# Input projection of a two-block transformer kernel: four panels multiplied by the unnormalised input

## The chip, the cores and the metric

The kernel is one program on one core of a Trainium2 chip. A core has a matrix engine (TensorE, PE in the profile), a vector engine (VectorE, DVE), a scalar engine (ScalarE, ACT), a general engine (GpSimd, POOL) and a sequencer that issues most transfers (SyncE, SP). They run side by side and wait for each other through semaphores. The metric is the device time of one execution in microseconds (us), the median of several.

## The reference, cut to what matters

The kernel computes two transformer blocks over 512 tokens of width 1024. Only the head of the first one matters here: the input is normalised, multiplied by one wide weight matrix, and the parts of the product go into two attentions.

```python
def rms_norm(x, g):
    xf = x.astype(jnp.float32)
    y = xf * lax.rsqrt(jnp.mean(xf * xf, axis=-1, keepdims=True) + EPS)
    return (y * g.astype(jnp.float32)).astype(x.dtype)
...
        h = rms_norm(x, g_mix_pre[l])
        proj = h @ w_in[l]
        q_f, k_f, v_f, f_logit, q_c, k_c, v_c = jnp.split(proj, splits, axis=-1)
        log_f = jax.nn.log_sigmoid((f_logit + b_fgate[l]).astype(jnp.float32))
        o_f = fox_attention(...)
        o_c = chunked_rel_attention(...)
        o_f = rms_norm(o_f.reshape(B, S, FOX_WIDTH), g_fox_out[l])
        o_c = rms_norm(o_c.reshape(B, S, CHUNK_WIDTH), g_chunk_out[l])
        mix = jnp.concatenate([o_f, o_c], axis=-1) @ w_out[l]
        x = x + rms_norm(mix, g_mix_post[l])
```

## The kernel before

The activations lie transposed: a chunk of x is 128 channels by 512 tokens, and there are 8 chunks. Every product is made of three fp32r matmuls (lines 1029 to 1031): each operand is split into a rounded high part and the low rest, and high times high, high times low and low times high are added up. The weights come as panels of 128x1024 (512 KB), one panel for one output chunk: SP loads a panel into one of two slots of `stage`, ACT rounds it into `WH` (line 1763), POOL subtracts to get `WL` (line 820) and counts it in `s_split`. The third and fourth panel of this projection go into a buffer of their own, `WX`. The load of panel p waits until panel p-2 is split.

At the start SP issues x in three parts (2, 2 and 4 chunks), the first constants, the vectors (gains, biases), panels 0 and 1, and, when all of x is there, the other constants (`con`), the condition and the gate weights. ACT squares the chunks of x (line 1791), DVE adds the squares (line 2485), PE sums them over the channels with a matrix of ones (lines 1157 and 1160), ACT takes the logarithm and the exponential (lines 1806 and 1809), which gives the reciprocal root. DVE scales a chunk (line 2515), ACT rounds it (line 1815), DVE makes its low part (line 2509): the pair is `H`. Meanwhile PE multiplies constants that nobody reads (`warm`, line 1136), 40 ahead of the sum and 14 behind it.

Then PE runs the input projection (`project`): output chunks 0 and 1 together, chunk of H by chunk of H, then chunks 2 to 15 one after the other, 24 matmuls each. Chunks 0 and 1 use the banks G[0] and G[1], 2 and 3 use ST and AD, all later ones G[0] and G[1] in turn. ACT copies a finished chunk rounded to `QKH` (line 1836), DVE makes `QKL` (line 2730) and so frees the bank. Beside the chunks each engine has other work, at fixed places between them: after chunk 0 ACT computes a SiLU of the condition between two loads of its function table (lines 2185 and 1800), after chunk 3 DVE subtracts over a bias table that SP loads when H is done (line 2943), and at every even chunk from 4 on DVE takes two pieces of another weight matrix (line 2574).

The values and gates follow, and then self attention, 64 steps over 16 heads. A step s is one head and one block of 128 queries; PE computes the scores of two heads together (lines 1344 to 1350, `score_pair`), DVE takes the maximum, ACT the exponential, PE transposes (line 1263, `turn`), ACT and DVE make the two parts of the transposed weights, and from step 8 on PE also multiplies them by the values (`weigh`). PE's order is written out in `attention`: pairs 0 and 2, then for each s `turn(s)`, `score_pair(s+4)` at even s, and what is to be weighed. The other attentions have `warm(O[1], 4)` ahead of each of the first four steps, self attention has none.

## Time and profile before

| | us |
|---|---|
| median of 3 runs | 2083.13 |
| lowest and highest run | 2078.95, 2084.5 |
| the profiled execution, its own time | 2083.59 |
| its span, first to last instruction | 2081.8 |
| mean granted TensorE clock | 0.994 |

The rows further down are of this one execution. A page begins with the busy time of each engine; then come a table of the span in 40 slices, groups of instructions, and, asked of the trace, the instructions of a stretch in order of time. "Granted clock" is the share of TensorE's full speed that the chip gave it: 1.00 is 2.4 GHz and 0.50 is 1.2 GHz.

### The profile page before, as it was taken

How to read it: one execution, taken by the hardware profiler on the slowest of the kernel's cores; microseconds unless marked ns; L12 is line 12 of the kernel's file. 1: busy time of each engine (PE TensorE's matmuls, PEld its weight loads, DVE VectorE, ACT ScalarE, POOL GpSimd, SP SyncE). 2: the span in 40 equal slices, each digit the busy share in tenths (PEclk: the TensorE clock that was granted, in tenths of full speed). 3: DMA queues.
4: the chain of work that ended last, by engine and by line, in shares of the span. 5: the costliest groups of instructions: out<-in, count | busy, mean ns of one | idle time of the engine just before them, and what ended most of it. 6: DMA issues, size and time to landing. Idle time of an engine off the chain costs nothing.

```text
span 2081.8 us, 27861 instructions
## 1 busy us (share of the span) xinstructions
PE 2048.6 (98%) x9868; PEld 1685.8 (81%) x9868; DVE 1115.9 (54%) x1704; ACT 864.7 (42%) x1413; POOL 938.0 (45%) x478
## 2 busy tenths in 40 slices
PE   9999999999999999999999999999999999999997
PEld 7877887888888888787778888888777888888887
DVE  4525735236777776763485533434576635334345
ACT  5326864354222222533386323223475653232333
POOL 3444585552545454434244344444445752444443
PEclk9998999999999999999999999999999999999999
DMA  6530152224566664264223233333222032333332
GB/s 208 192 110 21 42 182 82 80 61 142 172 219 235 226 228 140 91 241 153 76 61 97 61 96 96 100 92 101 81 91 72 1 102 61 91 101 93 99 97 85
DMA packets 70325, 238.40 MB, mean 115 GB/s; under 512 B 7776, under 2 KB 11232, under 8 KB 70112
## 3 DMA queue, kind: packets, MB, share of 16 engines
q1 hardware_dynamic: 70240, 237.26, 35.4%
q8 instruction: 54, 0.88, 0.2%
q14 instruction: 31, 0.25, 0.0%
HBM read 231.20 MB, written 2.10 MB: 112 GB/s over the span
## 4 chain that ended last, share of the span: by engine, by line
PE 52%; issue 18%; POOL 7%; DVE 5%; ACT 3%; DMA 1%; POOLq 0%; DVEq 0%; ACTq 0%; SPq 0%
PE bank L1029 16%; PE bank L1031 16%; PE bank L1030 16%; POOL WL L820 5%; PE bank L1178 1%; PE bank L1151 1%; DMA stage<-panels 1%; DVE bank L2599 1%; PE bank L1263 1%; DVE acc L2485 1%; PE bank L1136 1%; POOL CW L967 0%; DVE x L2603 0%; DVE CPT L3060 0%; ACT CPT L2301 0%
## 5 line engine op out<-in xcount | busy, mean ns | idle before, releaser
L820 POOL TENSOR_TENSOR WL<-stage,WH 128x1024 fp32r<-128x1024 f32 x256 | 634.0, 2477 | 891.6 <-ACT WH L1763 886.4
L1763 ACT ACTIVATE WH<-stage 128x1024 fp32r<-128x1024 f32 x256 | 271.5, 1061 | 810.1 <-PE bank L1031 795.4
L1029 PE MATMUL bank<-H,WH 128*128 128x512 f32 (+1 forms) x1132 | 438.0, 387 | 3.2 <-DVE H L2509 2.2
L1031 PE MATMUL bank<-H,WL 128*128 128x512 f32 (+1 forms) x1132 | 437.0, 386 | 0.0
L1030 PE MATMUL bank<-H,WH 128*128 128x512 f32 (+1 forms) x1132 | 437.0, 386 | 0.0
L2839 DVE TENSOR_TENSOR Y<-bank,Y 128x512 f32<-128x512 f32 x328 | 215.8, 684 | 94.6 <-PE bank L1031 93.9
L1029 PE MATMUL bank<-HID,WH 128*128 128x512 f32 (+1 forms) x688 | 264.3, 384 | 0.1
L1030 PE MATMUL bank<-HID,WH 128*128 128x512 f32 (+1 forms) x688 | 264.2, 384 | 0.0
L1031 PE MATMUL bank<-HID,WL 128*128 128x512 f32 (+1 forms) x688 | 264.2, 384 | 0.0
L1029 PEld LDWEIGHTS bank<-H,WH 128*128 128x128 f32 x1132 | 212.6, 188 | 48.1 <-issue 4.0
L1031 PEld LDWEIGHTS bank<-H,WL 128*128 128x128 f32 x1132 | 212.6, 188 | 43.2
L1030 PEld LDWEIGHTS bank<-H,WH 128*128 128x128 f32 x1132 | 212.6, 188 | 42.9 <-issue 0.2
L2825 DVE SCALAR_TENSOR_TENSOR t<-bank,t 128x512 f32<-128x512 f32 x64 | 44.3, 692 | 266.9 <-ACT t L2086 266.8
L2574 DVE SCALAR_TENSOR_TENSOR ahead<-ahead,cond 128x1024 f32<-128x1024 f32 x102 | 175.5, 1771 | 9.0 <-DMA ahead<-ada 9.0
L2829 DVE TENSOR_TENSOR HID<-t,HID 128x512 fp32r<-128x512 f32 x86 | 121.5, 1412 | 65.9 <-ACT HID L2091 65.9
L1029 PEld LDWEIGHTS bank<-HID,WH 128*128 128x128 f32 x688 | 129.3, 188 | 25.7 <-POOL WL L820 0.3
L1031 PEld LDWEIGHTS bank<-HID,WL 128*128 128x128 f32 x688 | 129.3, 188 | 25.7
L1030 PEld LDWEIGHTS bank<-HID,WH 128*128 128x128 f32 x688 | 129.3, 188 | 25.6
L2730 DVE SCALAR_TENSOR_TENSOR QKL<-bank,QKH 128x512 fp32r<-128x512 f32 x40 | 27.4, 690 | 94.6 <-ACT QKH L1836 90.9
L2091 ACT ACTIVATE HID<-t 128x512 fp32r<-128x512 f32 x86 | 54.2, 630 | 57.3 <-DVE t L2825 51.6
L2740 DVE TENSOR_REDUCE stat<-bank 128x1 f32<-128x128 f32 (+3 forms) x112 | 52.7, 474 | 29.6 <-PE bank L1350 25.6
L1136 PE MATMUL bank<-onesr,identr 128*128 128x512 f32 x238 | 64.3, 418 | 1.2 <-DVE onesr L2920 1.2
(489 smaller groups left out, 3576.0 us busy)
## 6 DMA issues: line engine op xcount, KB each, us to landing
stage<-panels SPq DMA_DIRECT2D x296, 512.0 KB, 3.6
ahead<-ada SPq DMA_DIRECT2D x102, 512.0 KB, 5.3
RAW<-panels SPq DMA_DIRECT2D x18, 512.0 KB, 4.1
apiece<-ada SPq DMA_DIRECT2D x10, 512.0 KB, 5.3
x<-xT SPq DMA_DIRECT2D x3, 1024.0 KB, 8.4
CS<-QKH SPq DMA_DIRECT2D x18, 128.0 KB, 2.3
outT<-x SPq DMA_DIRECT2D x16, 128.0 KB, 1.7
CS<-QKL SPq DMA_DIRECT2D x12, 128.0 KB, 2.4
```

The lines of the kernel that those rows point to most:

```text
L820: pool.tensor_tensor(low_of(p, slot), stage[:, slot, :], high_of(p, slot).bitcast(F32), ALU.subtract).then_inc(s_split, 1)
L1029: pe.matmul(out, wh, rh, start=start, stop=False)
L1030: pe.matmul(out, wh, rl, start=False, stop=False)
L1031: return pe.matmul(out, wl, rh, start=False, stop=stop)
L1136: pe.matmul(out[:, :], identr[:, :], onesr[:, :].rearrange("p (a b) -> p a b", a=1).to_broadcast([P, 4, P]), start=True, stop=True)
L1763: act.activation(high_of(p, slot), stage[:, slot, :], ACT.Copy).then_inc(s_hisplit, 1)
L2091: act.activation(HID[:, slot, j, 0, :], t[:, j, :], ACT.Copy).then_inc(sm["high"], 1)
L2574: dve.scalar_tensor_tensor(source, source, 1.0, cond[:], ALU.mult, ALU.mult, accum_out=adac[:, column])\
L2740: dve.tensor_reduce(stat[:, b:b + 1], score_bank(name, s)[:, 0:w], AX, ALU.max, negate=True)\
L2825: ins = dve.scalar_tensor_tensor(t[:, j, :], up_banks[j][:, :], 0.0, t[:, j, :], ALU.max, ALU.mult)
L2829: dve.tensor_tensor(HID[:, slot, j, 1, :], t[:, j, :], HID[:, slot, j, 0, :].bitcast(F32), ALU.subtract).then_inc(sm["split"], 1)
L2839: dve.tensor_tensor(Y[:, m, :], (T + O)[m % 4][:, :], Y[:, m, :], ALU.add)\
```

## The change

The change has three parts.

**Input projection.** ACT and DVE first split x itself, times the gain, into H (`raw_high`, `raw_low`). PE multiplies panels 0 to 3 by this unnormalised H (`project_in`). The sum of squares goes between the products of panel 2. Chunks 0 to 3 are then multiplied by the reciprocal root per token in their banks (`scale_raw`, on DVE) before they are copied out. H is overwritten with the normalised x chunk by chunk as PE has used it, and output chunks 4 to 15 are computed from that. The warmers ahead are 26, and none stand behind the sum. Chunk 2 now lies in AD and chunk 3 in ST.

**Loads.** SP issues panel 0, the vectors, the first part of x, panel 1, the rest of x, the first constants. Panels 6 and 7 are loaded ahead of the bias table and not behind it and two pieces. The bias table waits for the normalised H.

**Self attention.** Six constant matmuls ahead of `turn(0)` and two ahead of `turn(2)`.

```diff
+SELF_CONSTANTS = (6, 0, 2, 0)
...
-            for at, part in enumerate(X_PARTS):
+            def load_x(at):
+
+                part = X_PARTS[at]
                 sp.dma_start(x[:, part.start:part.stop, :],
                              xT[part.start * P:part.stop * P, :].rearrange("(c p) t -> p c t", p=P))\
                     .then_inc(s_x[at], 16)
-                if at == 0:
-                    sp.dma_start(con[:, 0:CON["mask"]], cons[:, 0:CON["mask"]]).then_inc(s_ones, 16)
-            sp.dma_start(vec[:], vecs).then_inc(s_vec, 16)
-            for slot in range(2):
-                sp.dma_start(stage[:, slot, :], panels[slot]).then_inc(s_stage[slot], 16)
+
+            sp.dma_start(stage[:, 0, :], panels[0]).then_inc(s_stage[0], 16)
+            sp.dma_start(vec[:], vecs).then_inc(s_x[0], 16)
+            load_x(0)
+            sp.dma_start(stage[:, 1, :], panels[1]).then_inc(s_stage[1], 16)
+            load_x(1)
+            load_x(2)
+            sp.dma_start(con[:, 0:CON["mask"]], cons[:, 0:CON["mask"]]).then_inc(s_ones, 16)
             sp.wait_ge(s_x[2], 16)
...
-            plain(2, 6)
-            sp.wait_ge(s_h, row(MAKES, "x")[1])
+            plain(2, 8)
+            sp.wait_ge(s_h, before(MAKES, "x") + KC)
             sp.dma_start(Y[:, 0:4, :].rearrange("p a b -> p (a b)"), bias).then_inc(s_bias, 16)
             load_piece(0)
             load_piece(1)
-            plain(6, 8)
...
+            def project_in():
...
+                half = KC // 2
+                for p in range(2):
+                    pe.wait_ge(s_split, p + 1)
+                    for k in range(half):
+                        input_chunk("x_raw", k)
+                        product(p, G[p], k)
+                for k in range(half, KC):
+                    input_chunk("x_raw", k)
+                    for p in range(2):
+                        last = product(p, G[p], k)
+                        if k == KC - 1:
+                            last.then_inc(s_used, 1)
+                pe.wait_ge(s_split, 3)
+                for k in range(half):
+                    product(2, own_bank("w_in", 2), k)
+                    if k == 1:
+                        pe.wait_ge(s_ones, 16)
+                        mean_square("x")
+                pe.wait_ge(s_split, 4)
+                pe.wait_ge(s_log, first_of(LOG, "x") + 1)
+                for k in range(half):
+                    product(3, own_bank("w_in", 3), k).then_inc(s_raw, 1)
+                for k in range(half, KC):
+                    first, second = product(2, own_bank("w_in", 2), k), product(3, own_bank("w_in", 3), k)
...
+                for c in range(4, 6):
+                    chunk_of(c, "w_in", c, c % 2, H[:, :, 0, :], H[:, :, 1, :], S, "x" if c == 4 else None, evicted=c - 3)
+                with pe.Fori(3, 8) as i:
+                    for j in range(2):
+                        chunk_of(i * 2 + j, "w_in", i * 2 + j, j, H[:, :, 0, :], H[:, :, 1, :], S)
...
-                    if s < 4 and name != "self":
-                        warm(O[1], 4)
+                    if s < 4:
+                        warm(O[1], SELF_CONSTANTS[s] if name == "self" else 4)
...
-            warm(AD, 40)
-            pe.wait_ge(s_ones, 16)
-            mean_square("x")
-            warm(AD, 14)
-            project("w_in", 16, "x")
+            warm(AD, 26)
+            project_in()
...
+            used(PANEL0["w_in"], 0)
+            evacuate_scaled(0)
             for m in range(KC):
+                if m == 2:
+                    used(PANEL0["w_in"] + 1, 1)
+                if m < KC - 1:
+                    act.wait_ge(s_raw, m + 1)
+                else:
+                    act.wait_ge(s_used, 4)
                 high_chunk("x", m, scaled_in, hh, lambda m: col("zero"))
...
+            high_near(0)
+            for c in range(1, 4):
+                evacuate_scaled(c)
+                high_near(c)
...
+            def scale_raw(c):
+
+                dve.wait_ge(s_used, PANEL0["w_in"] + c + 1)
+                dve.tensor_tensor(own_bank("w_in", c)[:, :], own_bank("w_in", c)[:, :], rstd[:, :], ALU.mult)\
+                    .then_inc(s_qscaled, 1)
...
             await_rstd("x", added=True)
+            scale_raw(0)
+            evacuate_low("w_in", 0, QKH[:, 0, :], QKL[:, 0, :], 64 ** -0.5)
             make_scaled("x", xc, vcol("g_mix_pre"), hl, zero)
             dve.memset(RG[:].bitcast(F32), 0.0)
             dve.memset(RB[:].bitcast(F32), 0.0).then_inc(s_pad, 1)
             for c in range(16):
-                evacuate_low("w_in", c, QKH[:, c, :], QKL[:, c, :], 1.0 if c // 4 % 2 else 64 ** -0.5)
+                if 1 <= c < 4:
+                    scale_raw(c)
+                if c:
+                    evacuate_low("w_in", c, QKH[:, c, :], QKL[:, c, :], 1.0 if c // 4 % 2 else 64 ** -0.5)
```

What stands in a row on ACT before, from the reciprocal root to the copy of chunk 1 (line 1815 rounds H, 1763 a panel, 1836 copies an output chunk; the waits are semaphores):

```order
L1809 ACTIVATE bank<-logs 128x512 [waits mean_squares_log]
L1815 ACTIVATE H<-bank,vec 128x512 [waits scaled,vectors_loaded,ones_loaded]
L1815 ACTIVATE H<-bank,vec 128x512 [waits scaled] x4
L1763 ACTIVATE WX<-stage 128x1024 [waits panel0_loaded]
L1815 ACTIVATE H<-bank,vec 128x512 [waits scaled] x2
L1763 ACTIVATE WX<-stage 128x1024 [waits panel1_loaded]
L1815 ACTIVATE H<-bank,vec 128x512 [waits scaled]
L1763 ACTIVATE WH<-stage 128x1024 [waits panel0_loaded,panel_used]
L1836 ACTIVATE QKH<-bank 128x512
L2185 ACT_TABLE_LOAD
```

The same place on ACT now (1865 rounds the normalised H, 1811 a panel, 2247 copies a scaled output chunk):

```order
L1859 ACTIVATE bank<-logs 128x512
L1811 ACTIVATE WH<-stage 128x1024 [waits panel0_loaded,panel_used]
L2247 ACTIVATE QKH<-bank 128x512 [waits raw_product_scaled]
L1865 ACTIVATE H<-bank,vec 128x512 [waits scaled,raw_chunk_used] x2
L1811 ACTIVATE WH<-stage 128x1024 [waits panel1_loaded,panel_used]
L1865 ACTIVATE H<-bank,vec 128x512 [waits scaled,raw_chunk_used] x5
L1865 ACTIVATE H<-bank,vec 128x512 [waits scaled,panel_used]
L2264 ACT_TABLE_LOAD
L2264 ACTIVATE cond<-cond 128x1024 [waits condition_loaded]
L1848 ACT_TABLE_LOAD
L2247 ACTIVATE QKH<-bank 128x512 [waits raw_product_scaled]
```

The SiLU and its two table loads still stand ahead of the copy of chunk 1, and that copy now stands behind the whole of H.

What stands in a row on DVE now, from the end of H to the first pieces (2592 makes the last low parts of H, 3017 multiplies a chunk by the root, 2813 makes a low part and frees a bank, 3048 is the subtraction over the bias table, 2657 takes a piece):

```order
L2592 SCALAR_TENSOR_TENSOR H<-bank,vec,H 128x512 [waits input_high] x2
L3031 MEMSET RG 40x512 [waits input_split]
L3032 MEMSET RB 104x512
L3017 TENSOR_TENSOR bank<-bank,rstd 128x512 [waits panel_used,cond_ready]
L2813 SCALAR_TENSOR_TENSOR QKL<-bank,QKH 128x512 [waits chunk_high_evacuated]
L3017 TENSOR_TENSOR bank<-bank,rstd 128x512 [waits panel_used]
L3042 TENSOR_TENSOR wgateL<-wgate,wgateH 128x192 [waits gate_weights_high]
L3048 TENSOR_TENSOR Y<-Y 128x2048 [waits bias_loaded]
```

There the multiplication and the low part alternate for chunks 1, 2 and 3, and the subtraction over the bias table stands between the low parts of chunks 3 and 4.

What stands in a row on PE now at the start of self attention (1187 is a constant matmul, 1401 the last product of a score pair, 1395 the first of the next one):

```order
L1401 MATMUL bank<-maskr,identr 128x128 x2
L1187 MATMUL bank<-onesr,identr 128x512 [waits values_evacuated]
L1187 MATMUL bank<-onesr,identr 128x512 x5
L1395 MATMUL bank<-QKH 128x384 [waits self_exp]
```

Before, no constant stood there: the transposition followed the score pair at once.

## Rows read from the trace of the kernel before

**Rows 1.** The page: span, and busy us (share) xinstructions of two engines

```profile
span 2081.8 us, 27861 instructions
PE 2048.6 (98%) x9868; PEld 1685.8 (81%) x9868; DVE 1115.9 (54%) x1704; ACT 864.7 (42%) x1413; POOL 938.0 (45%) x478
```

**Rows 2.** Timeline of PE, start: start us, us, engine, line, op, out<-in, count [idle before]

```profile
1.25 12.19 PE L1136 MATMUL bank<-onesr,identr 128*128 128x512 f32 x40 [1.25 <-DVE onesr L2920]
13.71 1.10 PE L1157 MATMUL bank<-acc,con 128*128 128x512 f32 x2 [0.27 <-DVE acc L2485]
14.64 1.02 PE L1160 MATMUL bank<-sq,con 128*128 128x512 f32 x2
...
19.65 0.47 PE L1029 MATMUL bank<-H,WH 128*128 128x512 f32 x1 [0.79 <-DVE H L2509]
...
52.41 0.39 PE L1029 MATMUL bank<-H,WH 128*128 128x512 f32 x1
```

**Rows 3.** Timeline of ACT, start

```profile
15.70 0.69 ACT L1806 ACTIVATE logs<-bank,eps 128x512 f32<-128x512 f32 x1 [0.31 <-PE bank L1160]
16.42 0.60 ACT L1809 ACTIVATE bank<-logs 128x512 f32<-128x512 f32 x1
...
31.76 0.58 ACT L1836 ACTIVATE QKH<-bank 128x512 fp32r<-128x512 f32 x1
32.36 1.28 ACT L2185 ACT_TABLE_LOAD   x1
33.66 1.06 ACT L2185 ACTIVATE cond<-cond 128x1024 f32<-128x1024 f32 x1
```

**Rows 4.** Timeline of DVE, start

```profile
19.42 0.75 DVE L2515 SCALAR_TENSOR_TENSOR bank<-x,vec,bank 128x512 f32<-128x512 f32 x1
...
20.73 0.75 DVE L2515 SCALAR_TENSOR_TENSOR bank<-x,vec,bank 128x512 f32<-128x512 f32 x1
...
32.38 0.69 DVE L2730 SCALAR_TENSOR_TENSOR QKL<-bank,QKH 128x512 fp32r<-128x512 f32 x1 [2.72 <-ACT QKH L1836]
...
42.97 2.28 DVE L2943 TENSOR_TENSOR Y<-Y 128x2048 f32<-128x2048 f32 x1
```

**Rows 5.** Timeline of POOL, start

```profile
31.93 2.41 POOL L820 TENSOR_TENSOR WL<-stage,WH 128x1024 fp32r<-128x1024 f32 x1 [2.34 <-ACT WH L1763]
```

**Rows 6.** Transfers issued in the first 60 us: count, KB each, median us to landing

```profile
stage<-panels SPq DMA_DIRECT2D x10, 512.0 KB, 3.7
...
x<-xT SPq DMA_DIRECT2D x1, 1024.0 KB, 8.4
Y<-bias SPq DMA_DIRECT2D x1, 1024.0 KB, 5.6
```

**Rows 7.** Windows of 1 us: length, PE busy (x), granted clock, DMA share, GB/s

```profile
162.00:163.00 1.00, 0.00 (x0) 1.00 0.91 318
165.00:166.00 1.00, 1.00 (x5) 0.50 0.00 0
...
181.00:182.00 1.00, 1.00 (x6) 0.80 0.00 0
351.00:352.00 1.00, 0.00 (x0) 1.00 0.00 0
```

**Rows 8.** Timeline of PE, start of self attention

```profile
161.56 0.44 PE L1350 MATMUL bank<-maskr,identr 128*128 128x128 f32 x2
163.45 0.30 PE L1263 MATMUL bank<-con,t 128*128 128x128 f32 x1 [1.45 <-ACT t L1988]
...
165.24 0.43 PE L1263 MATMUL bank<-con,t 128*128 128x128 f32 x1
...
170.78 0.69 PE L1350 MATMUL bank<-maskr,identr 128*128 128x128 f32 x2
...
185.41 0.44 PE L1350 MATMUL bank<-maskr,identr 128*128 128x128 f32 x2
...
196.35 0.44 PE L1350 MATMUL bank<-maskr,identr 128*128 128x128 f32 x2
```

More of the change, by code:

```diff
@@ L513, in own_bank @@
         def own_bank(name, c):
-            return [ST, AD][c - 2] if name in JOINT and c in (2, 3) else G[c % 2]
+            if name in JOINT and c in (2, 3):
+                return ([AD, ST] if name == "w_in" else [ST, AD])[c - 2]
+            return G[c % 2]
         def q_panel(i):
@@ L1031, in three, with chunk_of @@
                 return pe.matmul(out, wl, rh, start=False, stop=stop)
-            def chunk_of(p, name, c, slot, high, low, width, fresh=None, part=range(KC)):
+            def chunk_of(p, name, c, slot, high, low, width, fresh=None, part=range(KC), evicted=None):
                 wh, wl = high_of(p, slot), low_of(p, slot)
@@ L1039, in chunk_of @@
                 else:
-                    if part[0] == 0:
+                    if evicted is not None:
+                        freed(pe, name, evicted)
+                    elif part[0] == 0:
                         bank_free(pe, name, c)
@@ L1830, in evacuate, with evacuate_high @@
                         act.activation(dest(i * 2 + j), G[j][:, :], func, scale=scale).then_inc(s_free, 1)
-            def evacuate_high(name, dest, scale, width=S, after=None):
-                for c in range(row(PROJ, name)[1]):
+            def evacuate_high(name, dest, scale, width=S, after=None, chunks=None):
+                for c in chunks or range(row(PROJ, name)[1]):
                     used(PANEL0[name] + c, c % 2)
```

65 lines of the change are left out of this document (49 added, 16 removed).

## The prediction, made before the changed kernel was run

> **What bounds the kernel now.** The page says it first: PE is busy for 98% of the span [rows 1], so only what shortens PE's own time, or closes one of its few gaps, moves the end. I read two stretches. The first is the start in the timeline of PE: constants and the sum of squares up to 18.9 us, the first useful product at 19.65, and from there a matmul each 0.227 us without a gap. 144 of them are six output chunks, and the seventh (chunk 6) begins at 52.41 [rows 2]: 32.76 us, or 5.46 per chunk. The second is the start of self attention, where the windows show the granted clock: PE does nothing from 162 to 163, and from before 165 until about 181.4 (a window at 0.80 is two fifths of slow time) the clock is 0.50, which is 1.2 GHz, though PE is busy all the time [rows 7]. PE waits there for ACT's first exponential until 163.45 [rows 8].
>
> **Part 1, the projection.** Chunk 6 is the first that the change leaves as it was: from it on each chunk costs PE the same 5.44 us with ACT and DVE idle in between, so the gain of this part is 52.41 less the time at which chunk 6 can begin now. The changed start, step by step:
>
> - Start. Panel 0 is now the first transfer: some 3.7 us [rows 6] after 0.74, then ACT 1.06 (any copy of 128x1024, as the SiLU's) and POOL 2.41 [rows 3, 5], so split near 8.0. The 26 constants last longer: 40 took 12.19 [rows 2], where the later ones run each 0.227, so 14 fewer end 3.2 earlier, near 10.1. The first product starts there, 9.5 us ahead of before. Panels 0 and 1 are 48 matmuls, 10.9 us, and end at 21.0. Raw H costs DVE 0.66 a chunk and keeps ahead of that.
> - Panel 2. SP waits for all of x. Its last part, 1 MB, took 8.4 us [rows 6]; issued near 3.3 behind somewhat more, it lands at 12. Then SP issues four transfers of 0.4 us each (constants, condition, gates, panel 2): panel 2 goes out at 13.4 with 1 MB ahead of it. Its landing takes between 3.7 (a panel alone) and 8.4; I take 5.0, nearer to the first and to the 5.6 that a whole MB takes [rows 6], so 18.4. ACT 1.06 and POOL 2.41 give 22.0. PE waits 1.0 us. **This is the softest term: every microsecond that the panel lands later or earlier moves all that follows, down to a gain of 1.0.**
> - The root. Two chunks of product are 1.4 us, the sum of squares is 1.95 (13.71 to 15.66) [rows 2], so it ends at 25.4. Logarithm 0.69, and now two exponentials of 0.60 where one stood [rows 3]: DVE has the root at 27.4, against 17.0 before.
> - Normalised H. DVE first multiplies chunk 0 by the root, ACT splits panel 4 and copies chunk 0, DVE makes the low part: 0.7 + 1.1 + 0.6, less overlap, ends at 29.6. Eight chunks of H then cost DVE 1.31 each (19.42 to 20.73) [rows 4]: 10.5 us, and with the last tail H is ready at 40.8. PE meanwhile does panels 2 and 3 until 34.9, and chunk 4, whose last product must wait for the last of H, until 41.6: 1.2 us of waits.
> - Chunk 5 writes over bank G[1], where chunk 1 still lies. Its copy stands on ACT behind the last of H (40.0) and behind the table load 1.28, the SiLU 1.06 and the second load 1.28 [rows 3]. ACT copies at 43.5 in 0.58, DVE's low part 0.69 [rows 4] frees the bank at 44.9. **PE waits 3.3 us.** This is the new wait of the change; the SiLU had stood under running products before.
> - Chunk 6 needs five freed banks. DVE, from 44.9: chunks 2 and 3 take 0.69 + 0.58 + 0.69 each with hand-overs, to 49.2; then the subtraction over the bias table, 2.28 [rows 4], to 51.4; then chunk 4's low part, to 52.1. The bias table is issued at 40.9 and lands 5.6 later [rows 6], at 46.5, in time; with two more pieces in flight it has 2.7 us to spare. Panel 6 is split only after ACT has copied chunk 3 (48.5): 49.5, and POOL 2.41 makes 52.0. Both say 52.2, while chunk 5 has ended at 50.4.
>
> So chunk 6 begins at 52.2 against 52.41: **0.2 us gained**. The 9.5 us of the early start go into waits of 1.0, 1.2, 3.3 and 1.8 and the 1.95 of the sum, which now lies between useful products. Loading panels 6 and 7 ahead counts nothing: they land long before ACT can round them, at 48.5. The pieces come later on DVE but are asked for at the same distance as before.
>
> The Trainium skill's page ScalarE: Activation LUTs says under "What ACT_TABLE_LOAD costs" that a switch is 1283 ns plus a drain of about 1380 ns. The trace agrees with the first number, not with the second: the SiLU starts 0.02 us after its load ends [rows 3]. By the page the chain through two loads would be 2.8 us longer, an estimate from its figure.
>
> **Part 2, the constants in self attention.** Six constants cost 6 x 0.227 = 1.36 us and stand in a gap: PE ends its second pair at 162.0 and the transposition starts at 163.45 [rows 8]. They first wait for ACT's copy of the values, which I put at 162.2 at the latest, so they end at about 163.55, 0.1 late. Two more, 0.45, stand where nothing waits: they cost their time. What they may return is the clock. If it stays at 1.00:
>
> - From 165.24 to 170.78 [rows 8] PE ran without a gap at 1.2 GHz: 5.5 us become 2.8. Less 0.45 and 0.1, this saves 2.2.
> - From the pair of step 8 to that of step 16, 14.63 us (170.78 to 185.41); the same distance one group later, at full clock and gapless, is 10.94 (185.41 to 196.35) [rows 8]. This saves 3.7. The early group has some 1.1 us fewer products by the values in it, and against them waits of about 1 us for DVE and ACT, which the slow clock had hidden; I take them as equal.
>
> Together **5.9 us**, all on PE's path, and what follows (memory, later layers) hangs on the same semaphores and moves with it.
>
> **The sum.** 2083.59 (the profiled execution, 0.46 above the median of the three runs) less 0.2 less 5.9 is 2077.5; against the median, 2077.0. That is 0.29%, right at the 0.3% (6.2 us) below which a measurement of this kernel can't tell it from no change.
>
> **The rivals.**
>
> - *The clock falls all the same.* For it: the six constants are followed by some 9 us in which PE runs only short transpositions and half-height score products, and at 1.2 GHz just such work, with PE busy, did not bring the clock back until products by the values had run. Against it: at 351 PE stood for over 1 us and the clock stayed [rows 7], and groups with the same mix hold it. If it falls two or three microseconds later, the gain is 0 to 3: 2080 to 2083.5.
> - The Trainium skill's page TensorE: Matmul & The Clock Gate says under "Part 4: PE-mode transpose" that a transposition does not count as PE-busy in the same way. By this rule the rival above holds, at its own time; the slow stretch agrees with it.
> - *The loads do better.* If panel 2 lands by 17.4, PE does not wait for it and everything up to chunk 6 is 1.0 earlier; with shorter hand-overs on ACT and DVE perhaps 2.3: 2074.7 to 2076.
> - *The new wait ahead of chunk 5 costs the clock.* PE stands for 3.3 us there; 1.45 us after light work were enough at 162. At the start of the program the slow phase cost 12.19 - 40 x 0.227 = 3.1 us [rows 2]. Chunk 5 has 1.8 us of slack before chunk 6, so 1.3 net: 2078.3.
> - *Slower.* The same mechanism at its worst: the clock falls in that wait and stays down as long as in self attention, some 17 us [rows 7], half of which is 8.5, less the slack 6.7; and the constants buy nothing. 2083.1 + 6.7 = 2089.8. It decides from the point where the slow phase outlasts chunk 5 by more than two chunks.
>
> **How the numbers follow.** Forecast 0.60 (2075.3 to 2079, panel 2 landing within 1.5 us of mine), clock falls all the same 0.15, loads do better 0.12, wait costs the clock but briefly 0.08, slower 0.05. Range: I leave out the slower case and the edges of its neighbours, 2074.5 to 2083.0. Faster by over 0.3% (below 2076.9): all of "better", half of the forecast, 0.42. Within 0.3%: the other half, the late fall and the brief one, 0.53. Slower by over 0.3%: 0.05.
>
> **What the profile after would show.** First product at 10.1. Waits of PE ahead of panel 2 (1.0, on POOL), at the end of chunk 4, ahead of chunk 5 (3.3, on DVE's low part of chunk 1) and ahead of chunk 6 (1.8), which starts at 52.2; DVE's subtraction over the bias table at 49.2. Self attention: granted clock 1.00 from 162 to 185, and the pair of step 16 some 6 us earlier. I am wrong if chunk 6 starts more than 2 us from 52.2, or if the clock shows 0.50 anywhere between 45 and 185.

## The result

| | before | changed |
|---|---|---|
| median of 20 runs each, us | 2080.09 | 2084.71 |
| lowest and highest run | 2077.21, 2084.5 | 2082.52, 2086.47 |
| profiled execution, its own time | 2083.59 | 2083.43 |
| its span | 2081.8 | 2081.5 |
| mean granted clock | 0.994 | 0.996 |

The ratio is 1.0019, 95% interval 1.0013 to 1.0025: slower by 0.19%, which is within the 0.3% of "no change", but 7.7 us above my 2077.0 and outside the range. The two profiled executions are alike to 0.2 us, the medians are not. The reason stands in the list of the 20 times: the runs of before lie in two groups, 12 of them from 2077.2 to 2080.5 and 8 from 2082.7 to 2084.5, and the execution whose trace I read was of the upper one. So were two of the three times that I had.

### The profile page after: what moved, and what is told of

It reads as the page before. It is cut to its first block, busy times and chain, and to the rows that moved or that the text cites. A ratio compares the mean times of both kernels' runs of the same rounds, so it can differ in the third digit from the quotient of the medians.

```text
span 2081.5 us, 27853 instructions
## 1 busy us (share of the span) xinstructions
PE 2042.0 (98%) x9848; PEld 1677.9 (81%) x9848; DVE 1126.8 (54%) x1716; ACT 871.4 (42%) x1422; POOL 939.8 (45%) x478
## 4 chain that ended last, share of the span: by engine, by line
PE 55%; issue 15%; POOL 6%; DVE 5%; ACT 4%; DMA 1%; POOLq 0%; DVEq 0%; SPq 0%; ACTq 0%
PE bank L1037 17%; PE bank L1038 17%; PE bank L1039 17%; POOL WL L828 4%; DMA stage<-panels 1%; PE bank L1202 1%; PE bank L1229 1%; PE bank L1314 1%; DVE acc L2568 1%; PE bank L1187 1%; DVE bank L2682 0%; POOL CW L975 0%; DVE CPT L3165 0%; ACT CPT L2384 0%; DVE Y L2922 0%
## 5 line engine op out<-in xcount | busy, mean ns | idle before, releaser
L1038 PEld LDWEIGHTS bank<-HID,WH 128*128 128x128 f32 x688 | 129.3, 188 | 25.4
L1187 PE MATMUL bank<-onesr,identr 128*128 128x512 f32 x218 | 58.4, 413 | 1.4 <-DVE onesr L3003 1.3
```

Source lines behind the costliest of these rows:

```text
L1038: pe.matmul(out, wh, rl, start=False, stop=False)
L1187: pe.matmul(out[:, :], identr[:, :], onesr[:, :].rearrange("p (a b) -> p a b", a=1).to_broadcast([P, 4, P]), start=True, stop=True)
```

## The profile of the changed kernel

In these lines a timeline row is: start us, us, engine, line, operation, out<-in, count [idle before <-what ended it]. The page is nearly that of before [rows 1]: PE is 6.6 us less busy by its records, DVE 10.9 and ACT 6.7 us more (H is now made twice, and four chunks are scaled in their banks).

```profile
span 2081.5 us, 27853 instructions
PE 2042.0 (98%) x9848; PEld 1677.9 (81%) x9848; DVE 1126.8 (54%) x1716; ACT 871.4 (42%) x1422; POOL 939.8 (45%) x478
```

**The start.** Timeline of PE, all rows with idle time up to chunk 6 and, at 26.16, the end of the sum of squares. They answer to [rows 2].

```profile
1.25 7.76 PE L1187 MATMUL bank<-onesr,identr 128*128 128x512 f32 x26 [1.25 <-DVE onesr L3003]
9.39 0.47 PE L1037 MATMUL bank<-H,WH 128*128 128x512 f32 x1 [0.39 <-DVE H L3011]
13.11 0.50 PE L1037 MATMUL bank<-H,WH 128*128 128x512 f32 x1 [2.10 <-DVE H L3011]
23.80 0.50 PE L1037 MATMUL bank<-H,WX 128*128 128x512 f32 x1 [0.69 <-POOL WX L828]
...
26.16 1.02 PE L1211 MATMUL bank<-sq,con 128*128 128x512 f32 x2
41.42 0.50 PE L1037 MATMUL bank<-H,WH 128*128 128x512 f32 x1 [0.35 <-DVE H L2592]
46.65 0.77 PE L1037 MATMUL bank<-H,WH 128*128 128x512 f32 x1 [3.34 <-DVE QKL L2813]
55.40 0.49 PE L1037 MATMUL bank<-H,WH 128*128 128x512 f32 x1 [0.34 <-POOL WL L828]
```

PE's wait of 2.10 at 13.11 is for the low part of the third chunk of raw H. ACT's high part of it came late, since ACT had waited until 7.56 for the first part of x, then rounded panel 1, and waited again until 10.38 for the second part. And the low part itself was slow: of the two instructions in the row of DVE that follows the first took 1.83 us instead of 0.75, beside POOL's split of panel 1 (timelines of DVE and of POOL; what that means comes further down).

```profile
11.23 2.49 DVE L3011 SCALAR_TENSOR_TENSOR H<-x,vec,H 128x512 fp32r<-128x512 f32 x2 [1.32 <-ACT H L2223]
```

```profile
10.15 2.36 POOL L828 TENSOR_TENSOR WL<-stage,WH 128x1024 fp32r<-128x1024 f32 x1 [2.01 <-ACT WH L1811]
```

The last row of PE's timeline is the price of the change: chunk 6 starts at 55.40 where it started at 52.41, **3.0 us later**, though the first product came 10.3 us earlier. Timeline of ACT in the same stretch (answers to [rows 3]): panel 2 is rounded at 20.22 and ACT had waited for its landing; the two table loads and the SiLU stand ahead of the copy of chunk 1, as forecast.

```profile
20.22 1.06 ACT L1811 ACTIVATE WX<-stage 128x1024 fp32r<-128x1024 f32 x1 [1.88 <-DMA stage<-panels]
...
41.52 1.28 ACT L2264 ACT_TABLE_LOAD   x1
42.81 1.06 ACT L2264 ACTIVATE cond<-cond 128x1024 f32<-128x1024 f32 x1
43.88 1.28 ACT L1848 ACT_TABLE_LOAD   x1
45.18 0.60 ACT L2247 ACTIVATE QKH<-bank 128x512 fp32r<-128x512 f32 x1
```

Then the split of panel 6 on POOL and what DVE ran beside it (timelines of POOL and of DVE):

```profile
51.11 4.15 POOL L828 TENSOR_TENSOR WL<-stage,WH 128x1024 fp32r<-128x1024 f32 x1 [14.34 <-ACT WH L1811]
```

```profile
50.73 2.28 DVE L3048 TENSOR_TENSOR Y<-Y 128x2048 f32<-128x2048 f32 x1
52.93 0.68 DVE L2813 SCALAR_TENSOR_TENSOR QKL<-bank,QKH 128x512 fp32r<-128x512 f32 x1
53.53 2.81 DVE L2657 SCALAR_TENSOR_TENSOR apiece<-apiece,cond 128x1024 f32<-128x1024 f32 x1
```

The split takes 4.15 us where it took 2.41 [rows 5]. DVE's subtraction over the bias table was under way when POOL was ready (51.11) and ended at about 52.9: 51.11 to 52.9 is 1.8, which is about all of 4.15 - 2.41 = 1.74. Then the piece, which started at 53.53 while POOL was running, took 2.81 where it takes 1.22 alone: it stands still until POOL is done at 55.3. Two engines, two instructions, and each time the one that came second waits for the end of the first. Not every instruction of DVE does: between the two, the low part at 52.93, one of whose inputs lies in a bank, took its usual 0.68 beside the same split. The three that waited or made POOL wait (the subtraction, the piece, the low part of raw H) read two inputs from SBUF, the on-chip memory in which x, H and the panels lie. The page SBUF — State Buffer of the Trainium skill says just this in its section "SBUF: two separate sides": the port pair that VectorE and GpSimd share is an exclusive lock, the one that starts first keeps it for the whole instruction and "the other fully blocks", among others when the VectorE instruction has two inputs in SBUF and the GpSimd one reads SBUF. The trace agrees, to 0.15 us.

The trace of before had shown it already (timeline of DVE): the same instruction on pieces 0 and 1, the first beside POOL's split of 48.31 to 50.71, the second behind it.

```profile
49.36 2.44 DVE L2574 SCALAR_TENSOR_TENSOR apiece<-apiece,cond 128x1024 f32<-128x1024 f32 x1
51.73 1.22 DVE L2574 SCALAR_TENSOR_TENSOR apiece<-apiece,cond 128x1024 f32<-128x1024 f32 x1
```

**Self attention.** Windows of 1 us (length, PE busy, granted clock, DMA share, GB/s), the answer to [rows 7]:

```profile
45.00:46.00 1.00, 0.00 (x0) 0.79 1.05 442
46.00:47.00 1.00, 0.35 (x1) 0.50 0.87 361
52.00:53.00 1.00, 1.00 (x5) 0.79 0.03 12
168.00:169.00 1.00, 1.00 (x7) 1.00 0.01 2
996.00:997.00 1.00, 1.00 (x3) 0.50 0.00 0
```

The clock falls to 0.50 in the new wait ahead of chunk 5 and comes back at 52.4, is at 1.00 all through self attention, and falls once more at 994 to 998, where the profile of before had 1.00. The rows of self attention (answer to [rows 8]: there the pairs of steps 8, 16 and 24 stood at 170.78, 185.41 and 196.35):

```profile
165.27 1.66 PE L1187 MATMUL bank<-onesr,identr 128*128 128x512 f32 x6 [0.17 <-ACT V L1996]
...
171.71 0.44 PE L1401 MATMUL bank<-maskr,identr 128*128 128x128 f32 x2
...
182.57 0.44 PE L1401 MATMUL bank<-maskr,identr 128*128 128x128 f32 x2
...
193.51 0.44 PE L1401 MATMUL bank<-maskr,identr 128*128 128x128 f32 x2
```

Self attention begins 3.10 us later than before (its second pair at 164.66 against 161.56) and at step 24 PE is 2.84 ahead: **5.94 us gained** against 5.9 forecast. From there to the end the lead shrinks from 2.84 to 0.3.

So three things had to be settled: whether the 5.94 belong to every run; what makes the 3.0 at chunk 6; and where 2.5 us go behind self attention, in code that the change doesn't touch.

## The experiments

Each is timed against the kernel of before on the same chip. Medians of before in the three series: 2079.8, 2079.5, 2079.3.

### The parts one by one

The constants alone, on the kernel of before:

```diff
-                    if s < 4 and name != "self":
-                        warm(O[1], 4)
+                    if s < 4:
+                        warm(O[1], (6, 0, 2, 0)[s] if name == "self" else 4)
```

> The kernel before with only the eight constants in self attention. Theory (the clock fall at self attention is a matter of chance from run to run: the runs of the kernel before lie in two groups, 2077.2 to 2080.5 and 2082.7 to 2084.5, and its profiled execution was of the upper one): the constants remove the upper group and cost 0.45 to 0.8 us in the lower one, so the runs lie at 2077.5 to 2081 in one group and the median is 0 to 2 us below that of the kernel before. Rival (the fall is there in each run): the median is 5 to 6 us below. In the profile the granted clock is 1.00 from 160 to 185 by both.

Measured: median 2077.90 (2075.97 to 2080.05, 11 runs), ratio 0.9991 (0.9982 to 1.0000). The upper group is gone. The profiled execution took 2076.91, with no window under 1.00 between the start and the end. Against it the kernel of before has 10 of its 33 runs of that series above 2082.6; the median of the other 23 is 2079.2. So the constants showed no cost there, where 0.45 to 0.8 was expected; that they gain 1.3 is not shown (in the last series the kernel with constants and longer code, further down, had 2079.0 against 2078.3 for the lower group of before).

The projection alone, on the changed kernel:

```diff
-SELF_CONSTANTS = (6, 0, 2, 0)
+SELF_CONSTANTS = (0, 0, 0, 0)
```

> The changed kernel with the eight constants in self attention taken out. Theory: chunk 6 of the projection begins near 55.4 as in the changed kernel, 3 us later than before, and self attention has its chance of a slow phase back: runs in two groups, one some 3 us above the lower group of the kernel before and one some 5.5 us above that; median 3 to 6 us above the kernel before. Rival (the projection's loss is made only by chance of the profiled execution): median within 1 us of the kernel before.

Measured: median 2085.11 (2083.17 to 2090.35, 10 runs), ratio 1.0026 (1.0014 to 1.0037), again in two groups, 2083.2 to 2085.5 and 2088.3 to 2090.4; the profiled execution, 2088.62, was of the upper one and shows 0.50 from 166 to 182. **The slow stretch of self attention comes by chance, in about a third of the runs. None of the 11 runs with the eight constants lies in an upper group, and in the other two thirds no clear gain or cost is left.**

### The wait ahead of chunk 5, and the split of panel 6

The wait filled with 14 matmuls whose results nobody reads, ahead of chunk 5:

```diff
                 for c in range(4, 6):
+                    if c == 5:
+                        for _ in range(14):
+                            pe.matmul(T[0][:, :], high_of(3, 1)[:, 0:P], H[:, 0, 0, :], start=True, stop=True)
```

> The changed kernel with 14 products that nobody reads (a panel's block by a chunk of H, into a free bank) between output chunks 4 and 5, where PE waited 3.3 us. Theory (POOL's slowed split of panel 6, 4.15 us beside DVE's subtraction, sets the start of chunk 6 in any case): granted clock 1.00 from 42 to 55, chunk 5 ends near 52.1, chunk 6 still begins at 55.0 to 55.4, and the median moves by less than 1 us. Rival (the slow phase in the wait is what costs): chunk 6 begins near 52.5 and the median falls by 2.5 to 3 us.

Measured: the clock is 1.00 from 45 to 52, PE ends chunk 5 early and waits for POOL instead:

```profile
46.68 0.47 PE L1037 MATMUL bank<-H,WH 128*128 128x512 f32 x1 [0.17 <-DVE QKL L2816]
55.40 0.49 PE L1037 MATMUL bank<-H,WH 128*128 128x512 f32 x1 [3.00 <-POOL WL L828]
```

Chunk 6 starts at 55.40 to the hundredth; median 2084.51 (2080.73 to 2086.54, 12 runs), ratio 1.0018 (1.0008 to 1.0027). So the slow clock in chunk 5 cost nothing, but only just: in the changed kernel that chunk took 8.4 us instead of 5.44 and ended at 55.06, 0.34 ahead of the start of chunk 6. The two hid behind each other, and mending either alone could win 0.34 at most. Nor was the slow phase gone here: it moved into the new wait of 3.0 us (granted clock 0.75 in the window from 56, 0.50 from 57 and 58, 0.54 from 59) and slowed chunk 6, and self attention begins 1.66 later than in the changed kernel (its second pair at 166.32 against 164.66).

The same with the subtraction over the bias table two chunks later:

```diff
-                if c == 3:
+                if c == 5:
                     dve.wait_ge(s_bias, 16)
```

> As the kernel with the filled wait, and DVE's subtraction over the bias table moved from behind chunk 3 to behind chunk 5. Theory: POOL's split of panel 6 has no subtraction beside it for its first 1.5 us, takes 2.4 to 3.4 us in place of 4.15 (the piece that now follows chunk 4 also reads two inputs from memory), and chunk 6 begins at 53.5 to 54.6, 0.8 to 1.9 us earlier than without the move; the median falls by as much. Rival (the split was slow for another reason, the loads that ran beside it): it still takes 4 us and chunk 6 begins at 55.3.

Measured: chunk 6 at 53.29, 2.1 us earlier (timeline of PE), and the split takes 2.38: it had stood still for DVE and for nothing else.

```profile
53.29 0.49 PE L1037 MATMUL bank<-H,WH 128*128 128x512 f32 x1 [1.28 <-POOL WL L828]
...
65.86 0.49 PE L1037 MATMUL bank<-H,WH 128*128 128x512 f32 x1 [1.39 <-POOL WL L828]
```

But the median moved by 0.7 only: 2084.02 (2080.61 to 2085.79, 12 runs), ratio 1.0016 (1.0007 to 1.0024). The second row says why: ACT has to round that table before it rounds panel 8, and the table is now late. Most of the gain was handed back 12 us on; at self attention 0.24 of it is left (164.42 against 164.66).

### The landing of panel 2, and the SiLU

```diff
+            sp.wait_ge(s_split, 1)
+            sp.dma_start(stage[:, 0, :], panels[2]).then_inc(s_stage[0], 16)
             sp.wait_ge(s_x[2], 16)
             sp.dma_start(con[:, CON["mask"]:NCON], cons[:, CON["mask"]:NCON]).then_inc(s_c, 16)
...
-            plain(2, 8)
+            load_panel(3, 1)
+            plain(4, 8)
```

> The changed kernel with panel 2 requested as soon as panel 0 is split (about 8.2 us), ahead of the rest of the constants, the condition and the gate weights; nothing else changed. My softest term was the landing of this panel: 18.4 forecast, 20.2 measured, and PE stood 0.7 us for its split. Theory: it now lands by 15, ACT rounds it as soon as its raw H is done (17.7), POOL has split it by 21.2 and PE no longer waits for it; the sum, the root and all that hangs on it come 0.7 to 2 us earlier, chunk 6 at 53.5 to 54.8 against 55.40, the median 2083 to 2084. Rival: x, which landed late too, sets the start (PE stood 2.1 us for raw H); then the panel's landing buys nothing and chunk 6 stays within 0.3 of 55.4.

Measured: ACT rounds panel 2 at 17.65 with no wait for it, PE has no wait between 12.5 and 39.8, chunk 5 starts at 45.06 and chunk 6 at 53.79, both 1.6 earlier; median 2082.73 (2078.60 to 2083.88, 11 runs), ratio 1.0007 (0.9998 to 1.0016). About 1.0 of the 1.6 is the panel's: PE's wait for raw H ended 0.6 earlier too, at 12.51, and it ended at 12.48 in the kernel with the late table, which does not ask for the panel early. The wait ahead of chunk 6 is now 3.0 us, the clock falls in it (0.50 at 54 and 55), and at self attention only 0.16 of the 1.6 is left (164.50). The 2.0 us in the median are therefore not this gain carried through.

```diff
-            load_ln_exp()
+            act.preload_act_table_set("silu_and_others")
...
+            act.wait_ge(s_c, 32)
+            act.activation(cond[:], cond[:], ACT.Silu).then_inc(s_cond, 1)
+            load_ln_exp()
             root("x")
```

(and the SiLU taken out of `high_near`, the memsets of RG and RB put ahead of DVE's wait for the root)

> The changed kernel with the SiLU and its table load moved into ACT's idle time ahead of the root (ACT starts the program on the SiLU's table and loads the one with logarithm and exponential behind it), and DVE's two memsets moved ahead of its wait for the root. Theory: ACT copies chunk 1 as soon as DVE has scaled it, chunk 5 starts at 44.0 instead of 46.65, the split of panel 6 starts 2.6 earlier; the root comes up to 0.7 later, since 2.3 of ACT's work and hand-over fill an idle time of 2.9. Chunk 6 between 52.8 and 53.5, the median 1.9 to 2.6 below the changed kernel's: 2082.1 to 2082.8. Rival: the wait ahead of chunk 5 is covered by the split of panel 6 whatever ACT does (it stays near 55), median 2084.7.

Measured: one table load instead of two stands in ACT's idle time ahead of the root; chunk 5 starts at 44.48 and chunk 6 at 53.20. Timeline of PE:

```profile
44.48 0.47 PE L1037 MATMUL bank<-H,WH 128*128 128x512 f32 x1 [1.22 <-DVE QKL L2812]
53.20 0.79 PE L1037 MATMUL bank<-H,WH 128*128 128x512 f32 x1 [3.00 <-POOL WL L828]
```

The median is 2082.70 (2078.89 to 2083.99, 11 runs), ratio 1.0006 (0.9997 to 1.0015), 2.0 less than the changed kernel. The clock fell in the 3.0 us wait and was back at 57; chunk 6 ran its first 2.8 us at half the clock, which cost 1.4: its offset against the kernel with the constants alone grows from 0.8 to 2.3, and 2.25 of that are still there at self attention.

### Behind self attention

The fall at 994 followed small matmuls (128x8) of the gates. Four wide ones among them:

```diff
             for tt in range(NT):
                 for st in range(tt + 1):
                     pe.matmul(ST[:, tt * 8:tt * 8 + 8], upper[:, 0:P] if st == tt else ones, gz[:, st, :],
                               start=st == 0, stop=False)
                 last = pe.matmul(ST[:, tt * 8:tt * 8 + 8], ident, gi[:, tt, :], start=False, stop=True)
+                if tt == NT - 1:
+                    last.then_inc(s_row, 1)
+                pe.matmul(AD[:, :], H[:, 0, 0, 0:P], H[:, 0, 0, :], start=True, stop=True)
-            last.then_inc(s_row, 1)
```

> The changed kernel with four matmuls of 512 columns, results unused, among the 128x8 matmuls of the gates of the second mixer (990 to 993 us), behind which the granted clock fell to 0.50 for 3 to 4 us in the four profiles so far of kernels with the changed projection, and in neither profile of kernels with the projection of before. They cost 4 x 0.227 = 0.9 us. Theory: the light matmuls are what lets the clock fall; it stays at 1.00 from 990 to 1003, which returns 1.3 to 1.6; median 0.4 to 0.7 below the changed kernel's, 2084.1. Rival: the fall there is not decided by these matmuls (the same ones ran in the kernel of before without it); the clock falls all the same and the median is 0.9 higher, 2085.6.

Measured: the theory is wrong. The clock falls all the same, behind the wide ones (windows as above):

```profile
994.00:995.00 1.00, 1.00 (x8) 1.00 0.00 0
995.00:996.00 1.00, 1.00 (x4) 0.62 0.00 0
997.00:998.00 1.00, 1.00 (x4) 0.50 0.00 0
```

Median 2085.71 (2085.27 to 2087.70, 7 runs), ratio 1.0028 (1.0017 to 1.0040): their 0.9 us more, and nothing back.

All mends together. Beside those shown, ACT rounds panel 6 as soon as chunk 4 is done:

```diff
             for c in range(1, 4):
+                if c == 2:
+                    used(PANEL0["w_in"] + 4, 0)
                 evacuate_scaled(c)
```

> All mends together on the changed kernel: panel 2 early, SiLU and memsets early, panel 6 rounded by ACT as soon as chunk 4 is done (ahead of the copies of chunks 2 and 3), the subtraction over the bias table two chunks later, the four matmuls among the gates. Theory: POOL has split panel 6 by 47, so chunk 6 only waits for freed banks: it starts at 49.5 to 50.5, 2 to 3 us ahead of the 52.41 of the kernel before. If the later losses of the changed kernel (about 2 us of small waits, and the clock at 994) go with the late start, the median is 2075.5; if they belong to something else in the change, 2078 to 2079. Slower than the constants alone (2077.9) would say that the early start can't pay even with its waits removed.

Measured: chunk 6 at 50.08, 2.3 ahead of before, and then what the late table had cost above. Timeline of ACT:

```profile
57.34 1.92 ACT L2279 ACTIVATE XH<-Y 128x2048 fp32r<-128x2048 f32 x1 [6.25 <-DVE Y L3055]
59.17 1.04 ACT L1816 ACTIVATE WH<-stage 128x1024 fp32r<-128x1024 f32 x1
```

PE stands 1.49 us for panel 8 at 62.79; at 107 the lead is 0.2. Median 2082.61 (2079.96 to 2085.25, 11 runs), ratio 1.0012 (1.0003 to 1.0021): some 4.5 us above the constants alone, with self attention no later, and above both of the ranges that I expected (2075.5, 2078 to 2079). So the loss behind self attention does not need the late start.

Is it made by the place of the code? In the kernel with the constants alone, one pair of chunks written out ahead of the loop, 48 instructions of PE more, the same work in the same order:

```diff
                     first = 2
+                    if name == "w_in":
+                        for j in range(2):
+                            chunk_of(p0 + 4 + j, name, 4 + j, j, H[:, :, 0, :], H[:, :, 1, :], S)
+                        first = 3
```

> The kernel of before with the constants in self attention (2077.9) and, in the input projection, one more pair of chunks written out ahead of the loop instead of in it: the same matmuls in the same order at the same time, but 48 more instructions in PE's program ahead of all later code. The changed kernel has about as many more (6095 rows of instructions against 6048). Open is why the changed kernel and its mended forms lose 2 to 5 us behind self attention (at 330, 467, 994, 1126, 1690 us) that the kernel with the constants alone does not lose, though the code there is the same. Theory: where the code lies in memory decides the small hand-overs and with them where the clock falls; then this kernel loses part of it too: 2079.5 to 2082. Rival: it follows from the timing of the changed start; then this kernel stays within 0.8 us of 2077.9.

Measured: 2079.00 (2077.33 to 2081.60, 12 runs), ratio 0.9991 (0.9982 to 1.0001). And with longer programs of DVE and ACT too:

```diff
+            for j in range(9):
+                dve.memset(RB[0:8, 8 * j:8 * j + 8].bitcast(F32), 0.0)
             add_squares("x")
...
+            for j in range(6):
+                act.activation(logs[:, j:j + 1], eps[:, :], ACT.Copy)
             squares("x", xc, ...)
```

> As the one before, and 9 tiny memsets on DVE and 6 tiny copies on ACT in the idle time at the start, so that the programs of DVE and ACT are longer by as many instructions as in the changed kernel. In the changed kernel DVE began 0.46 us after ACT's exponential at 330 us, where it is 0.10 in the kernel with the constants alone. Theory of code position: this hand-over becomes 0.4 to 0.5 here, and the median 2080 to 2082. Rival: it stays 0.10, median within 0.8 us of 2077.9.

Measured: 2079.56 (2077.36 to 2081.07, 12 runs), ratio 0.9994 (0.9985 to 1.0002); the hand-over at 330 is 0.11, as in the constants alone. Both profiles show the clock at 0.50 at 988 to 994 and at 991 to 994. The medians lie 1.1 and 1.7 above the constants alone, but the ratios, each against before in its own series, can't be told from its 0.9991. Neither theory of the time is settled by this. Two things fall: that longer programs make the hand-over at 330 longer, and that the dip near 990 belongs to the changed start.

The mends once more, without the four matmuls, and with the table's subtraction ahead of pieces 0 and 1:

```diff
-                if c >= 4 and c % 2 == 0:
+                if c > 4 and c % 2 == 0:
                     piece(c - 4)
                     piece(c - 3)
                 if c == 5:
                     dve.wait_ge(s_bias, 16)
                     dve.tensor_tensor(nearf, ...).then_inc(s_near, 1)
+                    piece(0)
+                    piece(1)
```

> All mends without the matmuls among the gates, and with the subtraction over the bias table as DVE's first work behind the low part of chunk 5, ahead of pieces 0 and 1. In the form before it stood behind these pieces; ACT, which waits for it, then rounded panel 8 late and PE stood 1.5 us at 62.8. Theory: chunk 6 starts at 50.1 and no wait follows; self attention starts 2.3 ahead of the kernel with the constants alone. If the later losses follow from the timing of the start, the median is 2076 to 2078; if they come with the changed code whatever its timing, 2079.5 to 2081.5.

Measured: median 2077.92 (2076.28 to 2080.65, 12 runs), ratio 0.9989 (0.9979 to 1.0000). It is as fast as the constants alone, and by the two ratios (0.9989 and 1.0019) 0.30% or 6.2 us faster than the changed kernel. Self attention begins at 159.30, which is 5.36 ahead of the changed kernel, so nearly all of the 6.2 is the start. It is also 2.26 ahead of the constants alone (161.56), and of that lead 0.2 is left at the end of the profile: 0.4 goes at 344, where PE waits 2.17 for the last sum, and some 1.6 in a fall of the clock at 345 to 348. That the median fell into the range of my first branch says less than it seems to: I had not counted the lead in. The later losses of the changed code show in this profile too; in the medians 2.3 us is within the two intervals. Timelines of PE (its last wait up to self attention), POOL and DVE:

```profile
49.93 0.50 PE L1040 MATMUL bank<-H,WH 128*128 128x512 f32 x1 [0.59 <-DVE QKL L2818]
```

```profile
50.52 2.40 POOL L831 TENSOR_TENSOR WL<-stage,WH 128x1024 fp32r<-128x1024 f32 x1 [3.48 <-ACT WH L1814]
```

```profile
51.57 3.50 DVE L3053 TENSOR_TENSOR Y<-Y 128x2048 f32<-128x2048 f32 x1
54.99 1.21 DVE L2662 SCALAR_TENSOR_TENSOR apiece<-apiece,cond 128x1024 f32<-128x1024 f32 x1
```

Here POOL came first and ran its 2.40; DVE's subtraction, ready at 51.57, is longer by 1.22 (3.50 against 2.28), which is about the 1.35 that POOL still had to run. In the changed kernel it was the other way round. Which of the two pays is decided by who starts first.

Last, the kernel of before again, for a second profile:

> The kernel of before, unchanged, for a second profile. Its runs lie in two groups, about 2076.4 to 2080.5 and 2082.4 to 2084.5, and the profile that I predicted from was of the upper one. Theory: in the lower group the clock stays at 1.00 in self attention without any constants, so this profile (two chances in three) ends about 5.5 us earlier with no window under 1.00 from 160 to 185, or, if it is of the upper group, shows the same slow stretch again. A fall near 346 or 990 would show that these come by chance in the kernel of before too; the profile before had none. Rival: the groups differ by something else, and self attention is slow in either.

Measured: 2083.70, again of the upper group. Its windows (the columns as above):

```profile
163.00:164.00 1.00, 0.81 (x3) 0.50 1.08 382
179.00:180.00 1.00, 1.00 (x4) 0.50 0.00 0
180.00:181.00 1.00, 1.00 (x7) 0.99 0.00 0
997.00:998.00 1.00, 1.00 (x4) 0.50 0.00 0
```

Self attention is slow as in the first, some 1.5 us earlier in its onset and in its end, and the fall near 995 is there too, in the kernel of before. No profile of before in its lower group was had; that the clock holds there without constants is inferred, from two things. The constants reduce the groups to the lower one. And the mean granted clock of each run, which is on record for 91 runs of before in the three series, is 0.993 to 0.995 above 2082 us and 0.996 to 0.998 below, with three exceptions near the border; 17 us at half the clock are worth 0.004 of the mean.

## Why the prediction was wrong, step by step

My 2077.0 was 7.7 us too low. Of that, to 0.1, 3.2 is chunk 6 (55.40 where I had 52.2), 2.6 is lost behind self attention (the lead shrinks from 2.84 to 0.27), 1.3 is what the median lies above the profiled execution, and 0.5 is what I took off for the median of before. Against before I was off by more, 10.7 us (6.1 faster forecast, 4.6 slower measured): the other 3.0 is the median of before, 2083.13 in the three runs that I had and 2080.09 in twenty. The two signs by which I would be wrong both came: chunk 6 more than 2 us off, and the clock at 0.50 between 45 and 53.

- **Start.** First product forecast at 10.1, measured 9.39. The mechanism was not the forecast one: the 26 constants took 7.76 us and not 9.0, since the slow phase at the start of the program was shorter, and the product then waited 0.39 for raw H. That the time came out within 0.7 is in part luck.
- **Panels 0 and 1.** I let raw H keep ahead of PE. It didn't: PE stood 2.1 us at 13.11, 1.1 of it because DVE's low part stood still for POOL's split of panel 1. Here this wait cost nothing more, since PE then stood for panel 2 all the same; with panel 2 asked for earlier it is the wait that counts.
- **Panel 2**, the step that I had called the softest, was ready for ACT at 20.22 and not 18.4, and split 1.8 later. So the sum ended at 27.2 instead of 25.4, and every later step up to chunk 5 is 1.5 to 1.8 late: root 29.1 (27.4), H ready 42.3 (40.8), chunk 5 at 46.65 (44.9).
- **The wait ahead of chunk 5.** Forecast 3.3, measured 3.34. The mechanism (table load, SiLU, table load ahead of a copy) and its size were right, and moving it brought 2.2 us at chunk 5.
- **Chunk 6.** Forecast 52.2, measured 55.40. 1.75 is the lateness above. The rest is **the term that failed: POOL's split of panel 6 at 2.41**. I took the duration from a row where DVE did nothing large beside it, and in the same line of the text put DVE's subtraction over the bias table next to it. It was 4.15. My sentence "Both say 52.2" took the later of two chains as if they didn't hold each other up.
- **The clock in the wait ahead of chunk 5.** It fell, as in the rival with chance 0.08, and that rival's sum had it that it would cost 1.3. It made chunk 5 end at 55.06, 2.9 late, and cost nothing only because the split ended at 55.3. Without the stall on POOL, chunk 6 would have begun at 55.06 at best, so this term failed beside the other, hidden by it.
- **The constants.** Forecast 5.9, measured 5.94 between the two profiles, and in both parts: 2.2 up to the pair of step 8 (2.2 forecast), 3.8 from there to step 16 (3.7 forecast). From the trace that I started from, the constants alone give 2083.59 - 5.9 = 2077.7, and their median is 2077.90. What was wrong is to call it a gain over the median of before. Before lies in two groups some 4 to 5 us apart (5.3, 4.4, 3.7 and 5.3 by the medians of the groups in four series), and the slow stretch is in the upper one alone. The constants moved the median by 1.9 and the mean by 2.5. The range of the three runs, 2078.95 to 2084.5, was in front of me, as wide as the whole term; I compared the profiled execution to the median of three and not to the lowest run. Had I asked what differs between 2079 and 2084, the forecast for this part would have been near 0 against a run of 2079.
- **The later losses.** My sentence that what follows "hangs on the same semaphores and moves with it" put them at nothing, without a reason. Against the profile of the constants alone (span 2075.1) the changed kernel (2081.5) is 3.1 later at self attention and 6.4 at the end. The 3.3 between them: 0.4 at 346, where PE's wait for the last sum is 2.15 and not 1.73; 0.7 at 475, where a panel landed later and PE stood 0.80 for ACT's square; 0.4 won at 953; 1.6 for the fall near 994; 0.35 each at 1676 and 1700; 0.2 at the end. Their cause stays open. The result is slower, but by none of the mechanisms that I had named for it.

The 0.4 at 346 begins at a hand-over. DVE's next instruction follows the end of ACT's exponential, timelines of ACT and DVE of the constants alone, then of the changed kernel:

```profile
329.27 0.60 ACT L1809 ACTIVATE bank<-logs 128x512 f32<-128x512 f32 x1
329.97 0.76 DVE L2558 SCALAR_TENSOR_TENSOR bank<-Y,vec,bank 128x512 f32<-128x512 f32 x1 [10.11 <-ACT bank L1809]
```

```profile
332.46 0.60 ACT L1859 ACTIVATE bank<-logs 128x512 f32<-128x512 f32 x1
333.52 0.76 DVE L2641 SCALAR_TENSOR_TENSOR bank<-Y,vec,bank 128x512 f32<-128x512 f32 x1 [10.55 <-ACT bank L1859]
```

It is 0.10 to 0.11 us in the five profiles with the old projection and 0.45 to 0.46 in the nine with the new one, the ordered mends among them. I don't know why.

**What stays open.** The profiles show short falls of the clock at two places behind self attention, mostly 3.4 us long and some 1.7 us of lost time each; near 990 two of them are twice as long. Near 990: in eight of nine kernels with the changed projection and in three of five with the old one. Near 346: in four of the nine and none of the five; there PE waits longer by the hand-over above. The changed kernel's runs have no member below 2082.5, although the profile without its one costly fall would be 2081.8, so most of its runs lose more than the profiled one did; the median of the constants alone is 1.0 above a run without any fall. Where these runs lose it, and whether in more falls or in waits, is not shown: their mean clock is on record, 0.996 in 18 of 20 as in the profile, and is too coarse to tell. What makes the losses (the place of the code, the longer wait at 346, or chance between builds) is not settled either: the kernels with longer code don't decide it. Constants in the wait at 342 weren't tried, since no bank is free there.

## What to carry to other kernels

Before you subtract a slow phase of the clock from a median, look at whether the runs lie in groups and of which one the trace is; a phase that comes in a third of the runs is worth about a third of itself on average. When a duration of POOL is put into a sum, look at what DVE runs beside it at the new place, whether that reads two inputs from SBUF, and in which order the two start: the later one stands still until the earlier is done. When a wait and a slow clock end within 0.3 us of each other, as here, an experiment that takes away one of them shows nothing: take both away. And work that one engine moves out of the way (a table two chunks later) is late for whoever reads it: follow its reader's queue before counting the gain.

## What was not expected of the hardware

- DVE instructions with two inputs in SBUF and POOL's splits exclude each other for whole instructions: 2.41 became 4.15 on POOL; on DVE 2.28 became 3.50, 1.22 became 2.81 and 0.75 became 1.83, each time by what the other had left to run, to 0.2 us. DVE's low parts with one input in a bank were not held up (0.68 and 0.74 beside a split).
- The same kernel, at the same place, runs 17 us at half the clock in about a third of its runs (37 of 111 lie in the upper group). With six constants in the wait ahead (1.4 us) and two behind it, none of the 11 profiles shows a slow stretch there; that the clock is full in the other two thirds is inferred, as said above.
- The granted clock fell also with PE busy all the time, behind 3 us of 128x8 matmuls (near 990, in 11 of 14 profiles); four matmuls of 512 columns among them didn't prevent it.
- The table with the SiLU also serves Identity, Square and Copy: with it loaded first (at 0.73), ACT's rows up to the SiLU (at 24.18) show no further table load.
